# Attention that evicts turned probabilities ahead of exponents, and a memory norm inside the output product

## The reference, cut to what matters

```
u, q, k, v = project(modulate(x)); k_ctx, v_ctx = project(modulate(ctx))     # 8 heads of 64
s = concat(q.k_local*scale + bias(rpb), masked by column ; q.k_ctx*scale)    # 256 + 256 keys
attn = softmax(s) @ [v_local ; v_ctx]
mix  = concat(pool_mixer(u), attn) @ w_out
x    = x + gt1 * rmsnorm(mix)
y    = sq_relu_mlp(modulate(x)); x = x + gt2 * rmsnorm(y)
mem_k, mem_v = rmsnorm(mem_2) @ w_mem_kv_2                                   # 256 memory rows
```

## Time and profile before

| | |
|---|---|
| time, median of 3 runs | 1457.82 us (1457.36 to 1462.83) |
| the profiled execution: its time, its span | 1460.78 us, 1459.5 us |
| PE busy | 1368.8 us, 94% |
| PEld, DVE, ACT, POOL busy | 1088.9, 596.6, 546.5, 699.5 us |
| PE's granted clock over the span | 0.98 of full |
| values end, first scores of step 1 | 151.0, 151.75 us |
| last scores, first matmul of the output product | 209.78, 227.10 us |
| DVE begins the residual, PE begins the MLP | 286.56, 318.69 us |

### The profile page before, as it was taken

One profiled execution on the slowest core, in us unless ns is written; L12 is line 12 of the kernel. 1 busy time (PEld: TensorE's weight loads), 2 busy tenths in 40 slices (PEclk: granted clock), 3 DMA queues, 4 the chain that ended last, 5 costly groups with the idle time before them and its releaser, 6 DMA issues.

```text
span 1459.5 us, 16222 instructions
## 1 busy us (share of the span) xinstructions
PE 1368.8 (94%) x6458; PEld 1088.9 (75%) x6458; DVE 596.6 (41%) x836; ACT 546.5 (37%) x862; POOL 699.5 (48%) x375
## 2 busy tenths in 40 slices
PE   7999779888999999997999999999999999999999
PEld 4788557756888878886777777666677788888887
DVE  4795773483410043101747583854452211011110
ACT  4521563543433244322434535653343332122221
POOL 2544313744444434454458594443155654455542
PEclk9999999999999999999999999999999999999999
DMA  9564415222332323323221111211012333333232
GB/s 382 216 234 164 132 67 202 86 88 73 115 101 87 108 73 101 102 87 101 72 87 49 53 44 58 72 31 58 29 58 87 101 101 101 90 98 100 88 101 72
DMA packets 40651, 148.59 MB, mean 102 GB/s; under 512 B 4224, under 2 KB 4480, under 8 KB 39808
## 3 DMA queue, kind: packets, MB, share of 16 engines
q1 hardware_dynamic: 39696, 144.26, 30.4%
q0 software_dynamic: 448, 2.62, 0.5%
q10 hardware_dynamic: 432, 0.67, 0.1%
HBM read 144.65 MB, written 2.10 MB: 101 GB/s over the span
## 4 chain that ended last, share of the span: by engine, by line
PE 72%; DVE 11%; POOL 7%; ACT 5%; issue 4%; DMA 1%; SPq 0%; DVEq 0%; POOLq 0%; ACTq 0%
PE bank L543 20%; PE bank L544 20%; PE bank L545 20%; POOL wL L2380 2%; PE bank L592 2%; POOL EE L2526 2%; PE bank L599 1%; PE bank L580 1%; PE bank L582 1%; PE bank L581 1%; DVE xT L1980 1%; PE bank L882 1%; DVE acc L2085 1%; DVE y L1977 1%; PE bank L739 1%
## 5 line engine op out<-in xcount | busy, mean ns | idle before, releaser
L2380 POOL TENSOR_TENSOR wL<-raw,wH 128x1024 fp32r<-128x1024 f32 (+1 forms) x205 | 501.3, 2447 | 492.6 <-ACT wH L1152 492.5
L543 PE MATMUL bank<-hH,wH 128*128 128x512 f32 x784 | 321.8, 410 | 27.8 <-POOL wL L2380 10.7
L544 PE MATMUL bank<-hL,wH 128*128 128x512 f32 x784 | 311.3, 397 | 0.0
L545 PE MATMUL bank<-hH,wL 128*128 128x512 f32 x784 | 311.0, 397 | 0.0
L1152 ACT ACTIVATE wH<-raw 128x1024 fp32r<-128x1024 f32 (+1 forms) x205 | 214.4, 1048 | 219.8 <-PE bank L545 182.8
L543 PEld LDWEIGHTS bank<-hH,wH 128*128 128x128 f32 x784 | 151.0, 193 | 70.1 <-issue 31.5
L545 PEld LDWEIGHTS bank<-hH,wL 128*128 128x128 f32 x784 | 150.6, 192 | 33.2
L544 PEld LDWEIGHTS bank<-hL,wH 128*128 128x128 f32 x784 | 151.2, 193 | 30.0 <-issue 1.7
L543 PE MATMUL bank<-gH,wH 128*128 128x512 f32 x352 | 137.7, 391 | 5.6 <-POOL wL L2380 5.6
L545 PE MATMUL bank<-gH,wL 128*128 128x512 f32 x352 | 137.0, 389 | 0.0
L544 PE MATMUL bank<-gL,wH 128*128 128x512 f32 x352 | 137.0, 389 | 0.0
(11 more groups left out here) (345 smaller groups left out, 2053.0 us busy)
## 6 DMA issues: line engine op xcount, KB each, us to landing
raw<-in_wall SPq DMA_DIRECT2D x205, 512.0 KB, 3.6
rows<-in_wall SPq DMA_DIRECT2D x24, 1024.0 KB, 10.1
bra<-in_rpbw SPq DMA_DIRECT2D x8, 360.0 KB, 3.3
xq<-in_xt SPq DMA_DIRECT2D x2, 1024.0 KB, 6.8
xT<-in_xn SPq DMA_DIRECT2D x1, 2048.0 KB, 7.8
out_x<-xT SPq DMA_DIRECT2D x8, 256.0 KB, 2.2
vE<-in_ctxt SPq DMA_DIRECT2D x1, 1024.0 KB, 19.7
icn<-in_invc POOLq DMA_DIRECT2D x1, 1024.0 KB, 9.0
```

The source lines that it names most:

```text
L543: matmul(o, a_h, b_h, start=first, stop=False)
L544: matmul(o, a_h, b_l, start=False, stop=False)
L545: return matmul(o, a_l, b_h, start=False, stop=last)
L2380: tt(wL[i % NHL][:, 0:n], raw[i % NRAW][:, 0:n], wH[i % NHL][:, 0:n].bitcast(F32), ALU.subtract).then_inc(s.w_lo, 1)
```

## The change

ACT's iteration is now turned(i-2), exponent(i), out(i-3). The first step is normalized before the values are copied, and is turned and weighed among the first three steps of scores; the value copies are in another order (banks 4 and 5 first, then 2 and 3, then 0 and 1), and DVE's low parts come one iteration later. The last two turns and the last three value products stand inside the first two k of the output product, whose tiles 0 to 3 take banks 6, 0, 4 and 5, each claimed when its first matmul is due. The tables of heads 2 and 3 are loaded ahead of the shifted values, and POOL makes their bias ahead of the iterations. The memory is loaded when the last scores are done; its squares, sum and norm stand ahead of the output tiles on ACT, DVE and POOL, with the sum on PE behind k 5. DVE's last eight sums of w_mod follow the norm. A fifth `rows` buffer replaces the one that the norm would overwrite.

```diff
-ROW_PLACE = [p % NROW if p < 20 else 2 + p % 2 for p in range(PAIRS)]
+ROW_PLACE = [p % 4 if p < 20 else (2, 4)[p % 2] for p in range(PAIRS)]
...
-    turn(*(("w_out", m) for m in range(8)))
-    turn(*(("w_mem_kv_2", m) for m in range(4)), ("mem_v", 0), ("mem_v", 1))
+    of.update((("w_out", m), b) for m, b in enumerate((6, 0, 4, 5, 1, 2, 3, 6)))
+    of.update((("w_mem_kv_2", m), b) for m, b in enumerate((0, 4, 5, 1)))
+    of.update((("mem_v", i), 2 + i) for i in range(2))
+    n = 4
...
         value_rows_of_first()
-        for i in range(NEAR + 3):
-            if 0 < i < NEAR:
-                near_scores(i)
-            if 0 <= i - 2 < NEAR:
-                near_turn(i - 2)
-            if 0 <= i - 3 < NEAR:
+        near_scores(1)
+        near_turn(0)
+        near_scores(2)
+        near_values(0)
+        for i in range(3, NEAR):
+            near_scores(i)
+            near_turn(i - 2)
+            if i > 3:
                 near_values(i - 3)
...
+        def drain(k, m):
+
+            if (k, m) == (0, 1):
+                near_turn(NEAR - 2)
+                near_values(NEAR - 3)
+            if (k, m) == (0, 3):
+                near_turn(NEAR - 1)
+                near_values(NEAR - 2)
+            if (k, m) == (1, 3):
+                near_values(NEAR - 1)
+            if (k, m) == (2, 1):
+                late_columns(3, 4)
+            if (k, m) == (5, 3):
+                pe.wait_ge(s.add_v, ADD_V.m + 7)
+                statistic("mem", [(acc[1][:, 0:256], 0, 128)], 256)
+
+        group([("w_out", m) for m in range(4)], range(8), MX, drain)
...
@@ scalar_program
         for i in range(NEAR + 3):
+            if i == 1:
+                near_turned(0)
+            if 0 < i - 2 < NEAR:
+                near_turned(i - 2)
             if 0 < i < NEAR:
                 near_exponent(i)
-            if 0 <= i - 2 < NEAR:
-                near_turned(i - 2)
...
-        for m in range(4):
-            mixer_tile(m)
         act.wait_ge(s.mem_in, 16)
...
-        for m in range(4, 8):
+        ahead("w_out", 7, 0, 1)
+        root("mem", 1024, rs[0], 256)
+        for j in range(8):
+            act.wait_ge(s.full, FULL.hm + j + 1)
+            copy(hmH[:, j, :], tm[j % 2][:, 0:256], s.hi)
+        for m in range(8):
             ahead("w_out", 7, m)
-            if m == 5:
-                root("mem", 1024, rs[0], 256)
...
             mixer_tile(m)
...
@@ gpsimd_program
+        bias(2)
+        bias(3)
         for i in range(NEAR + 3):
...
-            if i % 4 == 1 and i < 12:
+            if i in (5, 9):
                 bias(i // 2 + 2)
                 bias(i // 2 + 3)
+            if i == NEAR:
+                pool.wait_ge(s.scores, 2 * NEAR)
+                nc.gpsimd.dma_start(xm[:, :, :], memt).then_inc(s.mem_in, 16)
...
@@ sync_program
             if i == first_out + 2:
+                bias_load(2)
+                bias_load(3)
                 sp.wait_ge(s.v_a, 3)
```

More of the change, by code:

```diff
@@ L406, in build @@
     xq = at("xq", Q, [128, 8, 512])
[L408 removed]
+    rows_ = [at("rows", at_, [128, 2, CB * 128]) for at_ in (0, 8 * K, Q + 18176, R + 46 * K, R)]
     mrow = [at("mrow", R + (24 + 2 * i) * K, [128, 512]) for i in range(2)]
@@ L564, in group @@
                 pe.wait_ge(sem, value)
-                for (name, m), o in zip(tiles, outs):
+                for name, m in tiles:
+                    o = (bank[BANK[name, m]] if n else claim(BANK[name, m]))[:, 0:width]
                     w_h, w_l, raise_ = weights(name, k, m)
@@ L683, in tensor_program @@
         first = [("w_in", m) for m in range(6)]
-        group(first, range(8), X1, [claim(BANK[t]) for t in first], other_quarters)
+        group(first, range(8), X1, other_quarters)
         for m in range(4):
@@ L803, in tensor_program @@
         kv = [("w_mem_kv_2", m) for m in range(4)]
-        group(kv, range(8), XM, [claim(BANK[t])[:, 0:256] for t in kv], mixer_statistic)
+        group(kv, range(8), XM, mixer_statistic, 256)
         for m in range(4):
@@ L825, in tensor_program @@
             if half == 0:
-                group([("w_mlp_in", m) for m in ms[:4]], range(8), X2, [claim(BANK["w_mlp_in", m]) for m in ms[:4]])
+                group([("w_mlp_in", m) for m in ms[:4]], range(8), X2)
                 for m in ms[:4]:
@@ L852, in tensor_program @@
         fs = [("w_in_2", m) for m in (10, 11, 12, 13)]
-        group(fs, range(8), X3, [claim(BANK[t]) for t in fs])
+        group(fs, range(8), X3)
         for h in range(4):
@@ L1113, in tensor_program @@
                 tiles = [("w_gate_2", 0), ("w_up_2", 0), ("w_gate_2", 1), ("w_up_2", 1)]
-                group(tiles, range(8), X4, [claim(BANK[t]) for t in tiles])
+                group(tiles, range(8), X4)
                 pe.wait_ge(s.add_g, ADD_G.x2 + 10)
@@ L1343, in scalar_program @@
                 held[t] = s.add_v, ADD_V.m + j
-        for m in range(4, 8):
-            ahead("w_out", 7, m)
-            if m == 5:
-                root("mem", 1024, rs[0], 256)
-                for j in range(8):
-                    act.wait_ge(s.full, FULL.hm + j + 1)
-                    copy(hmH[:, j, :], tm[j % 2][:, 0:256], s.hi)
+        ahead("w_out", 7, 0, 1)
+        root("mem", 1024, rs[0], 256)
+        for j in range(8):
+            act.wait_ge(s.full, FULL.hm + j + 1)
+            copy(hmH[:, j, :], tm[j % 2][:, 0:256], s.hi)
+        for m in range(8):
+            ahead("w_out", 7, m)
             mixer_tile(m)
@@ L1936, in vector_program @@
         nc.vector.tensor_copy(vC[:, 0, :], bank[4]).then_inc(s.v_v, 1)
+        nc.vector.tensor_copy(vE[:, 2, :], bank[2]).then_inc(s.v_v, 1)
         nc.vector.tensor_copy(vE[:, 0, :], bank[0]).then_inc(s.v_v, 1)
[L1938 to L1940 removed]
+        for i in range(1, NEAR + 4):
+            if i < NEAR:
                 near_top(i)
[L1942 removed]
+            if 0 < i - 1 < NEAR:
                 near_normalize(i - 1)
[L1944 removed]
+            if i % 4 == 3 and i > 3:
                 near_low(i // 4 - 1)
[L1948 to L1954 removed]
         for j in range(1, 8):
@@ L1971, in vector_program @@
                 rest(hmL[:, j - 1, :], tm[0][:, 0:256], hmH[:, j - 1, :], s.rest_v)
+        late_rows(8)
+        dve.wait_ge(s.mod_late, 3)
+        tt(coef[:, 2, :], mod[:, 16:24, 0], vcs("g_post_mix"), ALU.mult).then_inc(s.coef_b, 1)
+        stt(out=coef[:, 3, :], in0=mod[:, 32:40, 0], scalar=1.0, in1=vcs("g_pre_mlp"), op0=ALU.add,
+            op1=ALU.mult).then_inc(s.coef_b, 1)
+        late_vector(5)
         dve.wait_ge(s.root, rooted("mix"))
```

81 lines of the change are left out of this document (29 added, 52 removed).

## The result

| | before | after |
|---|---|---|
| time, median of 4 runs each | 1460.08 us (1457.36 to 1462.83) | 1446.73 us (1446.45 to 1449.9) |
| ratio, 95% interval | | 0.9913, 0.9886 to 0.9941 |
| the profiled execution: time, span | 1460.78, 1459.5 | 1446.45, 1445.2 |
| PE's granted clock over the span | 0.980 | 0.982 |
| scores 15 start | 209.78 | 197.28 |

The kernel is faster by 0.9%, 13.35 us in the medians. 1442.5 was forecast, 4.2 less than it takes. What follows goes by three landmarks: the start of scores 15, DVE's residual, and the end of the span. They gain 12.5, 11.0 and 14.3 us. So the attention carries the whole gain; from scores 15 to the residual the changed kernel takes 78.3 us where the old one took 76.8.

What follows compares the result with a forecast made beforehand. PE bounds the kernel except between 145 and 287 us, where engine chains make it wait. 8.9 + 3.75 + 7.9 - 8.5 + 4.1 = 16.2, less 0.7 for hand-overs, gives 1442.5 us against the median; range 1434 to 1451.

Steps and rivals of the forecast that it cites:

- Part 1: Attention, copies ahead of exponents: step 4's bias addition to scores 15 takes 36.2 us instead of 45.1, gain 8.9.
- part 2: Attention's start: DVE's bias addition of step 4 starts at 160.95 instead of 164.70, gain 3.75 us (2.5 to 4.5).
- the head-pair ends of part 1: Attention: three head-pair ends, where DVE's low part makes it late, cost 2.0 us in all.
- Part 3: Attention's tail moved inside the output product: removes most of 9.1 us idleness and half clock, gain 7.9 (6 to 9).
- Part 4: Norm inside the output product: PE waits 7.1 us for W4, slow clock adds 1.4; loss 8.5 (6.8 to 10.7).
- The clock behind it: Output product behind the W4 wait: matmuls at a lower clock cost 1.4 us, up to 2.9.
- Part 5: Output product's end to DVE's residual: 5.6 us instead of 9.7, gain 4.1 (3 to 4.5).
- The sign that I gave: After the output product: DVE's residual starts near 270 us, where it began at 286.56 before.
- B: Rival, attention: it gains little, held by small waits and clock dips, 6 to 7 us worse, 1449 us; chance 0.2.
- its worst end: Attention: head-pair ends cost as before and multiplications of `P` meeting POOL's bias cost about 1 us twice; 6 worse.
- A: Rival, output product: ACT gets to W4 in time, no wait, 8.5 us more gain, 1434 us; chance 0.1.
- D: Rival, output product: SP loads W7 behind `rows` loads that wait for DVE's late sums; slower, 1465 us; chance 0.04.

Runs made afterwards that it cites:

- Experiment 8: Kernel before with turned copies ahead of exponents, biases of heads 2 and 3 made early, DVE's low parts one iteration later; 1440.64 us, ratio 0.9854.
- experiment 4: Kernel before with only ACT's order changed: copies of turned(i-2) ahead of exponent(i); 1452.24 us, ratio 0.9926.
- 7: Kernel before with turned copies ahead of exponents and the early biases of heads 2 and 3; 1444.14 us, ratio 0.9885.
- experiments 2: Changed kernel with weight chunk W4 split and subtracted ahead of the norm on ACT and POOL; 1445.98 us, ratio 0.9883.
- 9: Changed kernel with the two column sums apart, and W4 and W5 split ahead of the norm; 1441.96 us, ratio 0.9878.
- experiment 11: Changed kernel with DVE's eight late sums moved ahead of the norm and their row loads one place earlier on SP; 1450.55 us, ratio 0.993.
- 6: Kernel before with only the biases of heads 2 and 3 loaded and made ahead of the loop; 1459.95 us, ratio 0.9988.

## Why the prediction was right, and where it was not

**Part 1 and 2, attention.** 12.65 forecast, 12.5 measured (197.1 forecast for scores 15, 197.28 found). Split where the prediction split it, at the bias addition of step 4 (found at 161.64, with no wait, forecast for 160.95), part 1 gave 9.4 for 8.9 and part 2 gave 3.1 for 3.75. The sum is right; the names on its terms are not. The order alone gives 4.6 and the early biases alone 0.2; with both it is 6.5, and with the late low parts 12.25. I wrote the low parts' delay into the head-pair ends of part 1 (2.0 for three) and never priced the edit that buys it: 5.75, measured under the new order and early biases. No term stands alone in such a loop, since each edit only uncovers the next engine that is late: ACT's copies, then POOL's bias, then DVE's idleness for the pair's copy. No run has the late low parts alone. Part 2's 3.75 was read from one bracket, though the earlier trace rows already told that PE's turns were as late.

**Part 3, the tail.** 7.9 forecast. Against the kernel before it came nearly true. From scores 15 to the last tile of the product the old kernel takes 67.1 us and the changed one 73.0 (197.28 to 270.28), 5.9 more. The waits for W4 and W6 (7.30 + 0.48), the slow matmuls behind W4 (1.95) and the column sums (3.1) are 12.8; so everything else in the stretch became 6.9 shorter, 1.0 less than forecast. What was wrong is to whom this belongs. I took 16.3 us of the old tail, subtracted PE's work and called the rest the move's gain. Experiment 8 moved no part of the tail and its stretch takes 62.6 (197.53 to 260.1): 4.5 of the gain came with the edits of the attention, 2.2 of it with the order (64.9 in experiment 4, 66.0 in 7) and most of the rest with the late low parts. In the changed kernel the moved tail itself then saved 2.4 (12.8 less the 10.4 that it takes longer than experiment 8). That is a remainder, since no run moved the tail without the norm. A second count agrees: at the first matmul of k 5, ahead of the norm and behind the same sums, the changed kernel is 0.4 later than experiment 8 from scores 15 on, and 3.1 of lateness is the merged sums', which leaves 2.7. The rows say where it comes from: 3.0 us of idleness in experiment 8 (0.72 + 2.28) and about 1.2 of half clock behind it, against 1.07 in the changed kernel.

**Part 4, the norm.** The wait: 7.1 forecast, 7.30 found, of the right engine at the right tile. The clock behind it: 1.4 forecast, 1.95 found, between my ends of 1.4 and 2.9. W6 cost 0.48 more, which I had at nothing. The contention that I added as 0.3 was 0.9 for the first subtraction (3.3 instead of 2.40), and it goes on for six operations of POOL, which is why taking W4 out of the wait (experiments 2, 9) only makes W5 and W6 late. The rule I cited from the Trainium skill, "SBUF — State Buffer", section "SBUF: two separate sides", gave 1.0 for it, and the trace and experiment 11 agree with that.

**Missed altogether:** the two column sums in one piece, 3.1 us, the largest single error. I had priced only their work.

**Part 5, after the product.** 5.6 forecast, 5.3 found (270.28 to 275.58), against 9.7: a gain of 4.4 for 4.1. It belongs to the moved norm, since experiment 8 with the old one takes 9.7. So in the changed kernel the norm cost 9.7 and gave 4.4 back, a loss of 5.3; with the sums' 3.1 and the tail's gain of 2.4 that is the 6.0 by which experiment 8 is ahead from scores 15 to the residual.

So from scores 15 to the residual I forecast a gain of 3.5, and there is a loss of 1.5. The 5.0 between them are the sums (3.1), the tail (1.0), the waits (0.7) and the clock behind W4 (0.5), less 0.3 for part 5. The sign that I gave, DVE's residual near 270, failed with it. The forecast of 1442.5 came out near by luck: behind the residual, 3.3 us came back that I had not counted (14.3 at the end of the span against 11.0). Nothing shows them to be the change's. Behind the two restarts of the MLP the gain still stands at 10.6: there nineteen matmuls are slow in the changed kernel and thirteen in the old. The old program behind the residual took 1172.9 us in the profile of the kernel before, and 1167.7 to 1173.2 in those of experiments 4, 6, 7 and 8, so 3.3 us lie within what one execution differs from another.

**The rivals.** B, that the attention gains little, did not come: the clock was full and most steps took 3.1 to 3.2. What part 1 had only in its worst end, multiplications of `P` that meet POOL's bias and cost about 1 us twice, did come (0.88 and 0.83 more); the sum held all the same, so something else in the walk was priced too high. A, no wait for W4, was wrong. Of D the mechanism was there: SP's queue stood behind the four `rows` loads for 26.93 us and ACT waited 2.57 for a weight at 255.19, which PE's slack covered. What I had no rival for was what the runs found: that a simpler part of the change would do better than the whole.

SP's queue and ACT's wait in the changed kernel:
```profile
221.71 26.93 SPq L2667 DMA_DIRECT2D rows<-in_wall  x4
```
```profile
255.19 1.06 ACT L1166 ACTIVATE wH<-raw 128x1024 fp32r<-128x1024 f32 x1 [2.57 <-DMA raw<-in_wall]
```

## What to carry to other kernels

Before an idle stretch is booked as the gain of the edit that fills it, ask what it will be once the other edits are in: here a tail in which nothing was moved shrank from 17.3 to 11.2 us by edits of the loop ahead of it, and filling it as well then saved 2.4 instead of 6.9. A serial chain of small steps (a norm) put in front of the weights of a running product made the product wait in every variant tried here, whichever weight was exempted. Of a wait, read the second releaser too: the one in the bracket may hide another a microsecond behind. And in a bundle, run the parts cumulatively as well as alone: the early bias is worth 0.2 us by itself and 1.9 behind the new order. Landmarks in the trace tell such edits apart where the time of the whole program, which varies by several us, does not.
